# hid turned without TensorE: moved between partitions by DMA, turned in 32x32 blocks by VectorE

## The chip, the core and the metric

The kernel runs on one core of one Trainium2 chip. The metric is the device time of one execution in microseconds (us). The core has five engines that run side by side, each through its own instructions in order: TensorE (PE, with its weight loads listed apart as PEld), VectorE (DVE), ScalarE (ACT), GpSimd (POOL) and SyncE (SP). SP only issues DMAs here. All DMAs, whoever issues them, are carried by the same 16 DMA engines of the core.

## The reference

One layer of an encoder is computed for two groups of 1024 tokens of width 1024: a mixer (mLSTM heads and neighbourhood attention), and then a mixture of 16 experts in which each expert picks the 128 tokens of a group that suit it best. The change touches only the experts:

```
xe  = xf[idx]                                    # 128 tokens of each group, for each expert
hid = silu(xe @ w_gate[e]) * (xe @ w_up[e])      # (128, 1024) for each group
ye  = (hid @ w_down[e]) * gate
y   = zeros.at[idx].add(ye)
```

All three weights of an expert are 1024 x 1024 in float32. The output is x + gate2 * RMSNorm(y).

## The kernel before

The part before the experts (function `front`) takes the first 1235 us and is not touched. In it GpSimd loads the tile `fr_v` (line 906) by DMAs onto 120 or 80 partitions, whose source has as its outermost dimension 3 or 2 rows of the grid, with 40 runs of 512 B each that follow each other in HBM. The experts (function `experts`) are computed one after another. For each expert TensorE makes three products, GATE, UP and DOWN. Each has 128 tokens of two groups as rows (GROUPS = 2) and 1024 columns, so that four PSUM banks of 128 x 512 (BK = 4) hold one product; there are two such sets of banks, which alternate (j).

Every float32 operand is split into a high and a low part of the type fp32r, and each product is made of three: hi x hi, hi x lo, lo x hi. A weight comes in four pieces of 1 MB (NP = 4): a piece is 256 rows of the weight, as 128 partitions x 2 rows. A piece goes through these steps:

- SP loads it into its slot of `wf` (line 2225), once VectorE has split the piece that was in the slot before;
- ScalarE writes `w_hi` (line 2367), once the piece has landed and TensorE is done with the piece four pieces earlier;
- VectorE writes `w_lo` (line 2492);
- TensorE makes 24 matmuls from it (line 2630).

So pieces pass in a fixed order: UP of expert e, GATE of e+1, DOWN of e, UP of e+1. The order is written out by hand in `body` of each engine; nothing is scheduled by a planner. Experts 0 to 7 run in a hardware loop (`over_experts`), 8 to 15 are written out. From expert 9 on each expert also carries a "window" of up to four units of output work: POOL loads rows of y and x1 (lines 2302 and 2303), ScalarE squares, VectorE scales and adds, POOL stores.

A product needs its left operand with the contracted index on the partitions. `hid` is made with tokens on the partitions, and so it has to be turned before DOWN. Before the change `turn_h` does that on TensorE: 16 transposes of 128 x 128 into PSUM (line 2641), in the middle of GATE of e+1, whereafter ScalarE writes `h_hi` from PSUM (line 2374) and VectorE `h_lo` (line 2498). The input rows `xe` are turned in the same way by `turn_x` (same line 2641) in the middle of UP. `silu` (line 2384) and `multiply` (line 2508) make `hid`.

Of the kernel before, what the change touches and what calls it, by code (L numbers as in the profile page):

```python
# [2088 lines left out]
def experts(nc, io):  # L2089
# [25 lines left out]
    mats = [io[f"w_expert_{n}"].rearrange("e (q a p) n -> e q p a n", p=P, a=PIECE) for n in ("gate", "up", "down")]  # L2115
    with ExitStack() as ctx:
# [54 lines left out]
        hid_ready = s.sem("hid_ready")  # L2171
        h_turned = s.sem("h_turned")
# [43 lines left out]
        def is_last(e, n=1):  # L2216
            return isinstance(e, int) and e >= NE - n

        @block.sync
        def _(sp):  # L2220
            def load(e, step, first=False):
                for q in range(NP):
                    if not first:
                        sp.wait_ge(w_lo_ready, ONE + piece(e, step, q) - NP + 1)
                    sp.dma_start(wf[:, q, :, :], mats[step][e, q]).then_inc(w_loaded[q], 16)

            load(0, GATE, True)

            for g in range(GROUPS):  # L2230
                sp.wait_ge(first_x[g], 16)

            def body(e, j):
                load(e, UP)
                if isinstance(e, int) and e == FIRST:
                    for g in range(GROUPS):
                        sp.dma_start(rows[:, g, :], mod_row[g, GATE2:GATE2 + 1, :].to_broadcast([P, D])).then_inc(rows_loaded, 16)
                if not is_last(e):
                    load(e + 1, GATE)
                load(e, DOWN)  # L2240

            over_experts(sp, body)
# [117 lines left out]
        def _(act):  # L2360
# [60 lines left out]
            def body(e, j):  # L2421

                ns = window(e)
                if is_last(e):
                    split(e, DOWN, range(0, 2))
                    turned_out(e, (h_hi, j), h_turned, h_hi_ready, range(0, 2))
                    split(e, DOWN, range(2, NP))
                    for n in ns:
                        square(n)
                    turned_out(e, (h_hi, j), h_turned, h_hi_ready, range(2, BK))  # L2430
                else:
                    split(e + 1, GATE, range(0, 2))
                    turned_out(e + 1, (x_hi[:, 1 - j], 1 - j), x_turned, x_hi_ready)
                    split(e + 1, GATE, range(2, NP))

                    split(e, DOWN, range(0, 1))
                    for n in ns[0:2]:
                        square(n)
                    split(e, DOWN, range(1, 2))
                    turned_out(e, (h_hi, j), h_turned, h_hi_ready)  # L2440
                    split(e, DOWN, range(2, NP))
# [17 lines left out]
        def _(dve):  # L2459
# [39 lines left out]

            def multiply(e, j, bs=range(BK)):  # L2500
# [42 lines left out]
            def body(e, j):  # L2543
                ns = window(e)
                if is_last(e):
                    multiply(e, j, range(0, 2))
                    split(e, DOWN, range(0, 2))
                    turned_out(e, h_hi, h_lo, j, h_hi_ready, h_ready, range(0, 2))
# [4 lines left out]
                    turned_out(e, h_hi, h_lo, j, h_hi_ready, h_ready, range(2, BK))  # L2553
                    for n in ns:
                        result(n)
                else:
                    split(e + 1, GATE, range(0, 2))
                    turned_out(e + 1, x_hi[:, 1 - j], x_lo[:, 1 - j], 1 - j, x_hi_ready, x_ready)
                    split(e + 1, GATE, range(2, NP))
                    multiply(e, j)  # L2560
                    split(e, DOWN, range(0, 1))
                    for n in ns[0:2]:
                        mean(n)
                    split(e, DOWN, range(1, 2))
                    turned_out(e, h_hi, h_lo, j, h_hi_ready, h_ready)
# [40 lines left out]
        def _(pe):  # L2606
# [58 lines left out]
            def body(e, j):  # L2665
                first, second = range(0, 2), range(2, NP)
                pe.wait_ge(silu_ready, ONE + e * BK + 2)
                if is_last(e):
# [7 lines left out]
                    pe.wait_ge(h_ready, ONE + e * BK + 2)  # L2676
# [3 lines left out]
                    pe.wait_ge(h_ready, ONE + e * BK + BK)  # L2680
                    for b in bs[1]:
                        products(e, DOWN, j, h_hi, h_lo, bs=range(b, b + 1))
                else:
# [10 lines left out]
                    pe.wait_ge(h_ready, ONE + e * BK + BK)  # L2694
# [83 lines left out]
```

## Time and profile before

| | |
|---|---|
| median of 3 runs | 2404.12 us (2403.29 to 2409.57) |
| span of the profiled execution | 2402.6 us |
| its time outside the span | not listed apart; the median run is 1.5 us above the span |
| PE busy | 2296.1 us, 96% |
| DVE, ACT, POOL busy | 1208.7, 1103.8, 603.2 us |
| experts | from about 1235 us to the end |
| one expert, experts 1 to 14 | 68.85 us |
| loads of `wf` for GATE, UP, DOWN, issue to landing | 4.9, 4.9, 5.8 us |

In the page, a line of part 5 gives a group of instructions: how often, the sum of busy time, the mean of one in ns, and behind the second bar how long its engine stood idle just before, and what ended that. A matmul's own duration (389 ns) is longer than the distance from one to the next (227 ns), since they are pipelined: what a matmul costs is read from starts.

### The profile page before, as it was taken

What the parts mean: (1) busy time and instruction counts of PE and PEld (TensorE: products, weight loads), DVE (VectorE), ACT (ScalarE), POOL (GpSimd) and SP (SyncE); (2) the same over time, 40 slices, a digit from 0 to 9 for tenths busy, and PEclk for the clock granted to TensorE, in tenths of its full rate; (3) what the DMA queues carried; (4) which work ended last, traced back from release to release, by engine and by line L of the source; (5) the groups of instructions that cost most, each with busy time, mean ns of one, the idle gap of its engine ahead of it and who ended that gap; (6) DMA issues with size and microseconds to landing.
All of it is one profiled execution on the core that took longest, in us unless ns stands there. A gap on an engine that the chain in (4) does not pass through costs nothing. (4 is left out here: it accounts for less than half of the span.)

```text
span 2402.6 us, 35196 instructions
## 1 busy us (share of the span) xinstructions
PE 2296.1 (96%) x13583; PEld 1915.1 (80%) x13583; DVE 1208.7 (50%) x1881; ACT 1103.8 (46%) x1828; POOL 603.2 (25%) x676
## 2 busy tenths in 40 slices
PE   6999999999999999999947999999999999999997
PEld 4679989777899897667736888888888888888886
DVE  3222334554413346665566555544445556666655
ACT  4223444655433436665543444444444455555552
POOL 3004342443133324430021011111110122222434
PEclk9999999999999999999978999999999999999999
DMA  8835445658454459764547566666666678888785
GB/s 319 259 107 182 145 160 185 191 150 185 122 194 141 162 177 249 228 180 158 170 189 263 204 211 221 214 226 210 207 203 231 216 268 309 322 308 291 284 302 175
DMA packets 239040, 511.49 MB, mean 213 GB/s; under 512 B 36981, under 2 KB 128005, under 8 KB 235825
## 3 DMA queue, kind: packets, MB, share of 16 engines
q1 hardware_dynamic: 190960, 394.78, 49.0%
q0 software_dynamic: 47936, 114.77, 16.0%
q8 instruction: 93, 1.52, 0.3%
q14 instruction: 51, 0.41, 0.1%
HBM read 415.32 MB, written 93.69 MB: 212 GB/s over the span
## 5 line engine op out<-in xcount | busy, mean ns | idle before, releaser
L2492 DVE TENSOR_TENSOR moe_w_lo<-moe_wf,moe_w_hi 128x2048 fp32r<-128x2048 f32 x192 | 439.5, 2292 | 456.6 <-ACT moe_w_hi L2367 450.0
L2367 ACT ACTIVATE moe_w_hi<-moe_wf 128x2048 fp32r<-128x2048 f32 x192 | 367.8, 1916 | 551.4 <-PE moe_acc L2630 550.5
L2630 PE MATMUL moe_acc<-moe_w_hi,moe_x_hi 128*128 128x512 f32 x1024 | 401.7, 392 | 0.9 <-DVE moe_x_lo L2498 0.6
L2630 PE MATMUL moe_acc<-moe_w_hi,moe_x_lo 128*128 128x512 f32 x1024 | 398.9, 390 | 0.0
L2630 PE MATMUL moe_acc<-moe_w_lo,moe_x_hi 128*128 128x512 f32 x1024 | 398.4, 389 | 0.0
L2630 PEld LDWEIGHTS moe_acc<-moe_w_hi,moe_x_hi 128*128 128x128 f32 x1024 | 192.3, 188 | 40.7 <-DVE moe_x_lo L2498 0.8
L2630 PEld LDWEIGHTS moe_acc<-moe_w_hi,moe_x_lo 128*128 128x128 f32 x1024 | 192.2, 188 | 40.3
L2630 PEld LDWEIGHTS moe_acc<-moe_w_lo,moe_x_hi 128*128 128x128 f32 x1024 | 192.4, 188 | 38.9
L1793 PE MATMUL banks<-fr_w_hi,fr_h_hi 128*128 128x256 f32 x768 | 223.2, 291 | 0.0
L1793 PE MATMUL banks<-fr_w_lo,fr_h_hi 128*128 128x256 f32 x768 | 217.0, 283 | 0.0
L1793 PE MATMUL banks<-fr_w_hi,fr_h_lo 128*128 128x256 f32 x768 | 216.9, 282 | 0.0
L1784 PE MATMUL banks<-fr_h_hi,fr_w_hi 128*128 128x512 f32 x496 | 204.3, 412 | 1.9 <-DVE fr_h_lo L1381 1.1
L2630 PE MATMUL moe_acc<-moe_w_hi,moe_h_hi 128*128 128x512 f32 x512 | 199.3, 389 | 0.0
L2630 PE MATMUL moe_acc<-moe_w_hi,moe_h_lo 128*128 128x512 f32 x512 | 199.2, 389 | 0.0
L2630 PE MATMUL moe_acc<-moe_w_lo,moe_h_hi 128*128 128x512 f32 x512 | 199.2, 389 | 0.0
L1784 PE MATMUL banks<-fr_h_hi,fr_w_lo 128*128 128x512 f32 x496 | 194.2, 392 | 0.0
L1784 PE MATMUL banks<-fr_h_lo,fr_w_hi 128*128 128x512 f32 x496 | 193.7, 390 | 0.0
L1030 ACT ACTIVATE fr_stage<-banks 128x512 f32<-128x512 f32 (+1 forms) x114 | 67.3, 590 | 271.9 <-PE banks L1784 146.2
L1362 DVE TENSOR_TENSOR fr_w_lo<-fr_w_raw,fr_w_hi 128x1024 fp32r<-128x1024 f32 x56 | 73.6, 1316 | 208.3 <-ACT fr_w_hi L1018 208.3
L906 POOL DMA_DIRECT2D fr_v<-scratch_vov x224 | 156.5, 740 | 81.9 <-PE banks L1963 80.6
L1793 PEld LDWEIGHTS banks<-fr_w_hi,fr_h_hi 128*128 128x128 f32 x768 | 146.8, 191 | 4.9 <-issue 4.8
L1793 PEld LDWEIGHTS banks<-fr_w_lo,fr_h_hi 128*128 128x128 f32 x768 | 147.0, 191 | 0.1
(294 smaller groups left out, 4083.4 us busy)
## 6 DMA issues: line engine op xcount, KB each, us to landing
moe_wf<-in_w_expert_gate SPq DMA_DIRECT2D x64, 1024.0 KB, 4.9
moe_wf<-in_w_expert_up SPq DMA_DIRECT2D x64, 1024.0 KB, 4.9
moe_wf<-in_w_expert_down SPq DMA_DIRECT2D x64, 1024.0 KB, 5.8
fr_w_raw<-in_w_units SPq DMA_DIRECT2D x28, 1024.0 KB, 7.2
fr_bias<-in_na_bias SPq DMA_DIRECT2D x16, 1520.0 KB, 11.1
fr_a_w<-in_w_ada POOLq DMA_DIRECT2D x16, 1024.0 KB, 9.0
scratch_qk_t<-fr_stage SPq DMA_DIRECT2D x64, 256.0 KB, 2.5
scratch_vov<-fr_stage SPq DMA_DIRECT2D x96, 128.0 KB, 2.2
```

The costliest lines, as they stand in the source:

```text
L906: pool.dma_start(v[j][p0:CHUNK, CH_AT[rb] + n, :], v_view[2, m, r0:r0 + k, cols_, :]).then_inc(nv_loaded[j], 16)
L1030: nc.scalar.activation(out, product, ACT.Copy).then_inc(evac_done, 1)
L1362: nc.vector.tensor_tensor(w_lo[:, h % 2, k, :], w_raw[:, h % 2, k, :], w_hi[:, h % 2, k, :].bitcast(F32), ALU.subtract).then_inc(w_lo_read ...
L1784: mm = nc.tensor.matmul(ps[:, b % 2, :], w[x1][:, slot, k, a * P:(a + 1) * P], h[x2][:, k, t * HALF:(t + 1) * HALF], start=start, stop=stop)
L1793: mm = nc.tensor.matmul(ps[:, b % 2, part * QW:(part + 1) * QW], h[x1][:, k, tile:tile + P], w[x2][:, slot, k, :], start=(k == 0 and i == ...
L2367: nc.scalar.activation(w_hi[:, q, :, :], wf[:, q, :, :], ACT.Copy).then_inc(w_hi_ready, 1)
L2492: nc.vector.tensor_tensor(w_lo[:, q, :, :], wf[:, q, :, :], w_hi[:, q, :, :].bitcast(F32), ALU.subtract).then_inc(w_lo_ready, 1)
L2630: mm = nc.tensor.matmul(acc[:, j, b, :], x[:, g, k, :], w[:, q, a, h * HALF:(h + 1) * HALF], start=(k == 0 and i == 0), stop=(k == KC - 1 ...
```

## The change

`hid` is turned for experts 0 to 14 without TensorE. SP issues 32 DMAs for each expert (`move_h`, 16 for each group): each moves 32 partitions (a quarter of the tokens) x 256 columns (1 KB, a quarter of the columns) from `hid` to another quarter of the partitions of `h_quarters`. Then partition quarter u holds the columns u*256 to u*256+255 of all tokens, and one VectorE instruction for each group turns 32 x 32 blocks into `h_raw`. ScalarE and VectorE make `h_hi` and `h_lo` from that, from SBUF, in two instructions of 128 x 1024 each instead of four of 128 x 512 from PSUM. `h_quarters` and `h_raw` lie in the memory of `h_hi` and `h_lo`.

The turned `hid` then has its columns in another order over the partitions, and the rows of `w_down` are loaded in the same order: partition u*32+c of piece q holds the rows u*256 + q*64 + 2c and the one behind it, two rows of 4 KB that follow each other in HBM. The last expert keeps the old way.

```
@@ weights
-    mats = [io[f"w_expert_{n}"].rearrange("e (q a p) n -> e q p a n", p=P, a=PIECE) for n in ("gate", "up", "down")]
+    by_chunk = [w.rearrange("e (q a p) n -> e q p a n", p=P, a=PIECE) for w in weights]
+    by_quarter = [w.rearrange("e (u q c a) n -> e q u c a n", u=4, q=NP, c=QT) for w in weights]
@@ SP
+                    rows = by_quarter[step] if step == DOWN and e < NE - 1 else by_chunk[step]
+                    sp.dma_start(wf[:, q, :, :], rows[e, q]).then_inc(w_loaded[q], 16)
+            def move_h(e):
+                for g in range(GROUPS):
+                    sp.wait_ge(hid_ready, ONE + e * BK + 2 * g + 2)
+                    for t in range(4):
+                        for u in range(4):
+                            sp.dma_start(h_quarters[u * QT:(u + 1) * QT, g, t, :],
+                                         hid[t * QT:(t + 1) * QT, g, u * 2 * P:(u + 1) * 2 * P]).then_inc(h_moved[g], 16)
...
-                load(e, DOWN)
+                    load(e, DOWN, qs=range(NP - 1))
+                    move_h(e)
+                    load(e, DOWN, qs=range(NP - 1, NP))
@@ ScalarE
+            def h_out(e):
+                for g in range(GROUPS):
+                    act.wait_ge(h_turned, ONE + e * GROUPS + g + 1)
+                    nc.scalar.activation(h_hi[:, g, :, :], h_raw[:, g, :, :], ACT.Copy).then_inc(h_hi_ready, 1)
...
-                    act.wait_ge(h_turned, ONE + e * BK)
+                    for g in range(GROUPS):
+                        act.wait_ge(h_moved[g], e * 16 * 16)
@@ VectorE
+            def turn_h(e):
+                for g in range(GROUPS):
+                    dve.wait_ge(h_moved[g], (e + 1) * 16 * 16)
+                    columns = h_quarters[:, g, :, :].rearrange("p t n -> p (t n)").rearrange("p (b c a) -> p b a c", c=QT, a=PIECE)
+                    turned = h_raw[:, g, :, :].rearrange("p m (t r) -> p t m r", t=4)
+                    nc.vector.transpose(turned, columns).then_inc(h_turned, 1)
...
-                    split(e + 1, GATE, range(2, NP))
+                    split(e + 1, GATE, range(2, 3))
                     multiply(e, j)
+                    split(e + 1, GATE, range(3, NP))
+                    turn_h(e)
                     split(e, DOWN, range(0, 1))
+                    h_out(e)
@@ TensorE
-                    products(e + 1, GATE, 1 - j, x_hi[:, 1 - j], x_lo[:, 1 - j], first)
-                    turn_h(e, j)
-                    products(e + 1, GATE, 1 - j, x_hi[:, 1 - j], x_lo[:, 1 - j], second)
-                    pe.wait_ge(h_ready, ONE + e * BK + BK)
+                    products(e + 1, GATE, 1 - j, x_hi[:, 1 - j], x_lo[:, 1 - j])
+                    pe.wait_ge(h_ready, ONE + (e + 1) * GROUPS)
                     products(e, DOWN, j, h_hi, h_lo)
```

SP's order for one of the written-out experts, before (`moe_wf` is the tile of loaded weights):

```order
L2225 DMA moe_wf<-in_w_expert_up 128x2x1024 x4
L2225 DMA moe_wf<-in_w_expert_gate 128x2x1024 x4
L2225 DMA moe_wf<-in_w_expert_down 128x2x1024 x4
L2225 DMA moe_wf<-in_w_expert_up 128x2x1024 x4
```

and now:

```order
L2235 DMA moe_wf<-in_w_expert_up 128x2x1024 x4
L2235 DMA moe_wf<-in_w_expert_gate 128x2x1024 x4
L2235 DMA moe_wf<-in_w_expert_down 128x1x2048 x3
L2242 DMA moe_h_quarters<-moe_hid 32x256 x32
L2235 DMA moe_wf<-in_w_expert_down 128x1x2048
L2235 DMA moe_wf<-in_w_expert_up 128x2x1024 x4
```

The 32 small DMAs stand between the third and the fourth piece of DOWN, and a piece of DOWN has one run of 2048 values for each partition instead of two of 1024.

VectorE's order for one of the last experts, from GATE's second half to the output units, before:

```order
L2492 TENSOR_TENSOR moe_w_lo<-moe_wf,moe_w_hi 128x2048 x2
L2508 TENSOR_TENSOR moe_hid<-moe_hid,moe_acc 128x512 x4
L2492 TENSOR_TENSOR moe_w_lo<-moe_wf,moe_w_hi 128x2048
L2512 TENSOR_SCALAR moe_parts<-moe_parts 128x1 x2
L2492 TENSOR_TENSOR moe_w_lo<-moe_wf,moe_w_hi 128x2048
L2498 TENSOR_TENSOR moe_h_lo<-moe_acc,moe_h_hi 128x512 x4
```

and now:

```order
L2522 TENSOR_TENSOR moe_w_lo<-moe_wf,moe_w_hi 128x2048
L2551 TENSOR_TENSOR moe_hid<-moe_hid,moe_acc 128x512 x4
L2522 TENSOR_TENSOR moe_w_lo<-moe_wf,moe_w_hi 128x2048
L2535 STREAM_TRANSPOSE moe_h_raw<-moe_h_quarters 128x4x8x32 x2
L2522 TENSOR_TENSOR moe_w_lo<-moe_wf,moe_w_hi 128x2048
L2540 TENSOR_TENSOR moe_h_lo<-moe_h_raw,moe_h_hi 128x1024 x2
```

The product of silu and UP now stands ahead of the split of GATE's last piece, the two transposes behind that split, and `h_lo` behind the split of DOWN's first piece.

TensorE's order in the middle of GATE, before, with the 16 transposes of `hid`, which are gone now (in their place matmul follows matmul):

```order
L2630 MATMUL moe_acc<-moe_w_hi,moe_x_hi 128x512
L2630 MATMUL moe_acc<-moe_w_lo,moe_x_hi 128x512
L2630 MATMUL moe_acc<-moe_w_hi,moe_x_lo 128x512
L2641 MATMUL moe_acc<-moe_parts,moe_hid 128x128 x16
L2630 MATMUL moe_acc<-moe_w_hi,moe_x_hi 128x512
```

The 48 matmuls of GATE behind these transposes now stand directly behind the first 48.

## Rows read from the trace of the kernel before

**Rows 1.** Page, part 5: VectorE's weight split, and TensorE's first group of matmuls

```profile
L2492 DVE TENSOR_TENSOR moe_w_lo<-moe_wf,moe_w_hi 128x2048 fp32r<-128x2048 f32 x192 | 439.5, 2292 | 456.6 <-ACT moe_w_hi L2367 450.0
L2630 PE MATMUL moe_acc<-moe_w_hi,moe_x_hi 128*128 128x512 f32 x1024 | 401.7, 392 | 0.9 <-DVE moe_x_lo L2498 0.6
```

**Rows 2.** Window over expert 6: length, PE, PEld, DVE, ACT, POOL, PEclk, DMA, GB/s

```profile
1721.80:1790.60 68.80, 68.80 (x321) 57.44 (x320) 34.69 (x24) 31.15 (x28) 9.88 (x7) 1.00 0.66 213
```

**Rows 3.** Timeline of TensorE in that expert: start, us, engine, line, operation

```profile
1745.37 0.39 PE L2630 MATMUL moe_acc<-moe_w_hi,moe_x_hi 128*128 128x512 f32 x1
...
1756.26 1.91 PE L2641 MATMUL moe_acc<-moe_parts,moe_hid 128*128 128x128 f32 x16
1757.92 0.48 PE L2630 MATMUL moe_acc<-moe_w_hi,moe_x_hi 128*128 128x512 f32 x1
1758.24 0.40 PE L2630 MATMUL moe_acc<-moe_w_lo,moe_x_hi 128*128 128x512 f32 x1
```

**Rows 4.** Timeline of VectorE and SP around the end of UP

```profile
1749.73 2.48 DVE L2508 TENSOR_TENSOR moe_hid<-moe_hid,moe_acc 128x512 f32<-128x512 f32 x4
```

```profile
1731.72 0.37 SPq L2225 DMA_DIRECT2D moe_wf<-in_w_expert_down  x1
1744.46 0.37 SPq L2225 DMA_DIRECT2D moe_wf<-in_w_expert_down  x1
```

**Rows 5.** SP's DMA issues: min/median/max ns, and two in a row by the timeline

```profile
L2225 SPq DMA_DIRECT2D moe_wf<-in_w_expert_down x64: 367/370/373, 1318.6 to 2349.2; - x64
L519 SPq DMA_DIRECT2D scratch_ends<-fr_b x4: 421/426/607, 108.4 to 555.7; - x4
108.41 1.07 SPq L519 DMA_DIRECT2D scratch_ends<-fr_b  x2
899.96 4.84 SPq L549 DMA_DIRECT2D fr_mx_raw<-scratch_mix_t  x4
```

**Rows 6.** DMA issues: KB each, median us from issue to landing

```profile
scratch_vov<-fr_stage SPq DMA_DIRECT2D x96, 128.0 KB, 2.2
fr_v<-scratch_vov POOLq DMA_DIRECT2D x160, 60.0 KB, 6.9
fr_v<-scratch_vov POOLq DMA_DIRECT2D x64, 40.0 KB, 7.7
```

**Rows 7.** Groups by form: VectorE and ScalarE operations on 128 x 1024 values

```profile
L2526 DVE TENSOR_TENSOR moe_fx<-moe_fx,moe_fy 128x1024 f32<-128x1024 f32 x26 | 31.9, 1226 | 2.3 <-issue 0.5
L1373 DVE TENSOR_SCALAR fr_x<-fr_x,fr_rms 128x1024 f32<-128x1024 f32 x16 | 11.3, 768 | 3.4 <-POOL fr_rms L792 3.4
L1670 DVE TENSOR_TENSOR fr_nd<-fr_nd,fr_rr 128x1024 f32<-128x1024 f32 x8 | 18.4, 2305 | 0.2
L2407 ACT ACTIVATE moe_zero<-moe_fy 128x1024 f32<-128x1024 f32 x26 | 27.6, 1063 | 12.7 <-DMA moe_fy<-scratch_y,moe_parts 10.9
```

**Rows 8.** DMA view: 1746.9 to 1749.9, then the whole of expert 6

```profile
DMA packets 318, 1.24 MB, mean 412 GB/s; under 512 B 16, under 2 KB 16, under 8 KB 318
```

```profile
DMA packets 3840, 14.68 MB, mean 213 GB/s; under 512 B 256, under 2 KB 256, under 8 KB 3840
```

**Rows 9.** A load of `fr_v` by GpSimd; 1035.30 to 1035.62; 0.32 us of a weight piece

```profile
1033.84 1.44 POOL L906 DMA_DIRECT2D fr_v<-scratch_vov  x2
```

```profile
DMA packets 63, 0.01 MB, mean 44 GB/s; under 512 B 60, under 2 KB 60, under 8 KB 63
```

```profile
DMA packets 13, 0.05 MB, mean 166 GB/s; under 512 B 0, under 2 KB 0, under 8 KB 13
```

**Rows 10.** Windows around two changes of TensorE's clock (columns as in Rows 2)

```profile
1273.37:1276.10 2.73, 2.73 (x13) 2.73 (x14) 2.49 (x7) 0.30 (x2) 0.30 (x2) 0.50 0.02 6
2387.30:2392.30 5.00, 0.00 (x0) 0.00 (x0) 2.84 (x4) 0.72 (x2) 1.94 (x3) 1.00 0.26 107
2392.40:2402.00 9.60, 0.00 (x0) 0.00 (x0) 0.00 (x0) 0.00 (x0) 0.31 (x1) 0.50 0.14 55
```

**Rows 11.** Timeline of GpSimd in expert 12: the first of the four loads that start the window

```profile
2152.06 0.59 POOL L2302 DMA_DIRECT2D moe_fy<-scratch_y  x1 [0.93 <-DMA scratch_y<-moe_ye,moe_parts]
```

More of the change, by code:

```diff
@@ L2146, in experts @@
         hid = s.sb("hid", [P, GROUPS, D])
+        with nc.sbuf_tensor("moe_h_quarters", [P, GROUPS, 4, D // 4], F32) as h_quarters:
+            pass
         h_hi = s.sb("h_hi", [P, GROUPS, KC, P], F32R)
+        with nc.sbuf_tensor("moe_h_raw", [P, GROUPS, KC, P], F32) as h_raw:
+            pass
         h_lo = s.sb("h_lo", [P, GROUPS, KC, P], F32R)
@@ L2171, in experts @@
         hid_ready = s.sem("hid_ready")
+        h_moved = [s.soft_sem(f"h_moved{g}") for g in range(GROUPS)]
+        last_h_turned, last_h_hi_ready, last_h_ready = (s.sem(f"last_h_{n}") for n in ("turned", "hi_ready", "ready"))
         h_turned = s.sem("h_turned")
@@ L2239, in body @@
                     load(e + 1, GATE)
-                load(e, DOWN)
-            over_experts(sp, body)
+                if is_last(e):
+                    load(e, DOWN)
+                else:
+                    load(e, DOWN, qs=range(NP - 1))
+                    move_h(e)
+                    load(e, DOWN, qs=range(NP - 1, NP))
+            for e in range(NE):
+                body(e, e % 2)
         @block.gpsimd
@@ L2429, in body @@
                         square(n)
-                    turned_out(e, (h_hi, j), h_turned, h_hi_ready, range(2, BK))
+                    turned_out(0, (h_hi, j), last_h_turned, last_h_hi_ready, range(2, BK))
                 else:
@@ L2436, in body @@
                     split(e, DOWN, range(0, 1))
+                    h_out(e)
                     for n in ns[0:2]:
                         square(n)
-                    split(e, DOWN, range(1, 2))
-                    turned_out(e, (h_hi, j), h_turned, h_hi_ready)
-                    split(e, DOWN, range(2, NP))
+                    split(e, DOWN, range(1, NP))
                     silu(e + 1, 1 - j)
@@ L2498, in turned_out, with h_out @@
                     nc.vector.tensor_tensor(part(lo), acc[:, j, b, :], part(hi).bitcast(F32), ALU.subtract).then_inc(done, 1)
+            def turn_h(e):
[4 more added lines that the diff above has]
+                    nc.vector.transpose(turned, columns).then_inc(h_turned, 1)
+            def h_out(e):
+                for g in range(GROUPS):
+                    dve.wait_ge(h_hi_ready, ONE + e * GROUPS + g + 1)
+                    nc.vector.tensor_tensor(h_lo[:, g, :, :], h_raw[:, g, :, :], h_hi[:, g, :, :].bitcast(F32),
+                                            ALU.subtract).then_inc(h_ready, 1)
             def multiply(e, j, bs=range(BK)):
@@ L2547, in body @@
                     split(e, DOWN, range(0, 2))
-                    turned_out(e, h_hi, h_lo, j, h_hi_ready, h_ready, range(0, 2))
+                    turned_out(0, h_hi, h_lo, j, last_h_hi_ready, last_h_ready, range(0, 2))
                     multiply(e, j, range(2, BK))
@@ L2552, in body @@
                         mean(n)
-                    turned_out(e, h_hi, h_lo, j, h_hi_ready, h_ready, range(2, BK))
+                    turned_out(0, h_hi, h_lo, j, last_h_hi_ready, last_h_ready, range(2, BK))
                     for n in ns:
@@ L2564, in body @@
                     split(e, DOWN, range(1, 2))
-                    turned_out(e, h_hi, h_lo, j, h_hi_ready, h_ready)
                     for n in ns[0:2]:
@@ L2650, in turn_h @@
                 pe.wait_ge(hid_ready, ONE + e * BK + bs[-1] + 1)
-                turn(hid, j, h_turned, bs)
+                turn(hid, j, last_h_turned, bs)
             bs = [range(2 * g, 2 * g + 2) for g in range(GROUPS)]
```

14 lines of the change are left out of this document (8 added, 6 removed).

## The prediction

> **What bounds the kernel now.** I read the window over one expert first. In the 68.80 us of expert 6 TensorE is busy for 68.80 at the full clock, and the other engines for half of it or less [rows 2]. The groups by line agree: the first group of matmuls stood idle for 0.9 us in 1024, while VectorE and ScalarE wait for TensorE [rows 1]. So from GATE of expert 0 to the last DOWN the time is the sum of what TensorE does, at 0.2267 us from matmul to matmul, and every step of the change is asked two things: does it take starts off TensorE, and does TensorE now wait.
>
> **What goes.** The 16 transposes of `hid` start at 1756.26 and the next matmul at 1757.92, 1.66 us, and that matmul takes 0.32 us to the next start instead of 0.23 [rows 3]. One turn costs 1.75 us, and 15 of the 16 experts lose it: 26.3 us. Nothing hid it, so all of it is gain if nothing is late in its place.
>
> **What must be in time.** I count from the end of UP, at 1745.37 [rows 3], called 0. GATE of e+1 is 96 matmuls, 21.8 us. `h_ready` used to be met well before it; now DOWN starts at +21.8 only if the whole way has been gone: product in VectorE, 32 DMA issues, landing, transpose, split of DOWN's first piece, two `h_lo`.
> - Product: four operations in 2.48 us [rows 4], 0.62 each. It no longer stands behind GATE's last split, so group 0 is done at about +1.6 and group 1 at +2.8.
> - Issues: the nearest row is a DMA of 32 partitions on SP. It takes 421 ns at best, and two in a row 1.07 us with one of them at 607 [rows 5], which leaves 0.04 between them: 0.465 us each, 14.9 us for 32. From below, a load of 128 partitions issues in 0.37 [rows 5], 0.41 with the gap: 13.1. I take 0.465, same partitions. The last one is issued at +16.1 to +16.6.
> - Landing: 2.2 us from issue for 128 KB, the nearest [rows 6]; here 32 KB that stay in SBUF, so 1.5 to 2.2, I take 2.2: +18.3.
> - Transposes of 128 x 1024: not in this trace. Bounds are 0.77 us (a one-input operation) and 2.31 (one with a spread operand); I take 1.2, the plain 128 x 1024 with two inputs [rows 7], since the operand here steps over two values.
> - Behind the second transpose on VectorE stand the split of DOWN's first piece, 2.29 [rows 1], and two `h_lo` at 1.23 [rows 7]. ScalarE's `h_hi`, 1.06, lies beside the split.
>
> With loads as they are this gives 18.3 + 1.2 + 2.3 + 2.4 = +24.2: TensorE waits 2.4 us, more than the 1.75 it saves.
>
> **The loads of DOWN.** A piece has the same 1 MB, but its source is now a pattern of four blocks (u), each of 32 partitions, 256 KB in one run, where it was 128 rows. What does the trace show of a source with a small outermost dimension? `fr_v` is loaded by GpSimd with 3 or 2 outermost rows onto 120 or 80 partitions. Of the one issued at 1033.84, when nothing else moves, 3 packets of 4 KB started in 0.32 us (63 less 60 small ones), though it has 120 partitions to write; in the first 0.32 us of a weight piece 13 started [rows 9]. And 40 KB with 2 rows land in 7.7 us, 60 KB with 3 rows in 6.9 [rows 6]: time goes by what each row's share is, not by the bytes. I read it so: the outermost dimension of the source sets how many of the 16 DMA engines carry a DMA. These are GpSimd's DMAs, and none of SP's in this trace has such a pair of patterns; that SP does the same is my main assumption. Then a piece of DOWN is carried by 4 engines.
>
> The Trainium skill, DMA: Bandwidth & Descriptors, section "Why a DMA increments its semaphore by 16 and not by 1", says it outright: both kinds of DMA use the largest number up to 16 that divides the slowest dimension of source and of destination. By it the number here is 4; without it the sum would be the one that ends in +24.2. The trace of `fr_v` agrees with it.
>
> What 4 engines make of it: in the busiest stretch 16 engines move 412 GB/s [rows 8], 25.75 each. A piece has 256 KB for each of 4, 10.2 us, instead of 64 KB for each of 16, 2.5.
> - Three pieces stand ahead of the small DMAs. The first is issued at 1731.72, -13.65, and the third at 1744.46, -0.9 [rows 4]. The first packets come 1.0 us later, since one follows the other without a gap: -12.7 + 30.5 = +17.9.
> - The same engines carry their share of gather and scatter. An expert moves 14.68 MB [rows 8], of which 12 pieces are 12.58, so 2.1 MB are GpSimd's; most of it (I take 1.8 MB, an estimate from the places of these DMAs in the expert) falls into this stretch: 1.8 / 16 / 25.75 GB/s = 4.4 us. Third piece done: +22.2.
 So some of the 32 are issued only afterwards. +25.7 if none, +29 if ten; I take +27.
> - Transpose 1.2, split 2.3, two `h_lo` 2.4: +32.9. TensorE waits 32.9 - 21.8 = 11.1 us.
>
> **The clock.** After the last matmul TensorE was still granted 1.00 for the 5 us to 2392.3, then 0.50 (1.2 of 2.4 GHz), and after a long pause it worked for its first 2.73 us at 0.50 [rows 10]. A wait of 11 us is longer than the 5.3 after which the level fell, so DOWN begins at half speed for some 2.7 us: 1.4 us lost. A wait of 2.4 us costs nothing of this kind.
>
> **Experts 9 to 14.** GpSimd issues four loads of 512 KB at the start of each window, at 2152.06 in expert 12 [rows 11], 6.4 us before the end of its UP (2134.89 + 23.56). They lie ahead of or between the third piece: 2 MB / 16 / 25.75 = 5.1 us more, a wait of 16.2.
>
> **The sum.** Experts 0 to 8: 11.1 + 1.4 - 1.75 = 10.75, times 9: 97. Experts 9 to 14: 16.2 + 1.4 - 1.75 = 15.85, times 6: 95. Together +192 on the span of 2402.6: 2595, and 1.5 more for what lies between span and median run: 2596 us. The last expert is unchanged.
>
> Check of the loads as a whole: each of the four engines carries in an expert 4 MB / 4 + 8 MB / 16 + (2.1 + 1.0) / 16, 1.77 MB, 69 us, and 84 with the window. The expert would last 79.6 and 84.7. So they are nearly saturated, and in the window the time could not be shorter by another route.
>
> What costs nothing: the fourth piece of DOWN comes late (issued at about +27, landed +39), and TensorE needs it three pieces after DOWN's start, +49. ScalarE's new order and the smaller reads (SBUF for PSUM) lie beside DOWN. SP's unrolled loop takes register steps away from an engine that waits.
>
> **Range of this case.** From below: no blocked issue, half of GpSimd's share, a transpose of 0.77: wait 7.1, 12.2 in windows, sum +133, 2537. From above: in expert 6 the engines are busy 0.66 of the time [rows 2] where 14.68 MB at 25.75 each need 0.52; if the three pieces are stretched by the same 1.27, 8.2 us, and the transpose takes 2.3: waits 20.4 and 25.5, +332, 2736.
>
> **Rivals.**
> 1. SP's loads use 16 engines all the same, and the chain of 32 issues is what is late. For it: the rows on `fr_v` are of another issuer, and the destination has 128 partitions. Wait 2.4, no clock loss: 15 x (2.4 - 1.75) = +10, 2414 us; with a transpose of 2.3, 2430.
> 2. The other side: 16 engines, and the way ends in time. It decides at +21.8, that is 2.4 us less than my sum. 0.41 for an issue gives 1.8 of them, a landing in 1.5 another 0.7. Then 2404.1 - 26.3 = 2378 us. Against it: each of these values is the lower bound of its row.
> 3. Four engines, but `hid` and the pieces do not queue behind each other as I have it, and only saturation counts: 9 experts at their wait of rival 1, +0.65 each, and 6 at 84 instead of 68.85, +15: 2502 us.
>
> **Chances.** Four engines as summed 0.67, rival 3 0.08, rival 1 0.15 (of which 0.03 within 0.3%), rival 2 0.10 (0.01 of it within). 0.3%, 7 us, is about what a measurement of this kernel tells from no change. So slower 0.87, same 0.04, faster 0.09. The predicted time is that of the likeliest, 2596 us; its own range 2537 to 2736. The range of 8 in 10 takes in rivals 3 and 1: 2405 to 2710.
>
> **What would show it.** In the profile after: `moe_wf<-in_w_expert_down` lands in some 12 us or more, while the other two stay near the 4.9 of the table; TensorE waits for `h_lo` at its first matmul of DOWN, 15 times, over 10 us each; the clock's row falls to 0.50 there; VectorE's largest idle time is ahead of the transposes, ended by the DMA of `h_quarters`. If DOWN's pieces land in 5 us, the step on four engines is wrong and rival 1 or 2 holds, told apart by whether that wait is there at all. If they land late and TensorE waits under 5 us, it is the queueing that I have wrong. The transposes' mean tells whether 1.2 us stood.

## The result, and the profile after

The changed kernel takes 2881.01 us (2866.86 to 2885.66, 4 runs), the kernel before 2403.82 us beside it: a ratio of 1.1972, interval 1.1941 to 1.2002. The prediction was 2596 us with a range to 2710. The sign was right; the loss is 477 us, not 192.

The page of the kernel after, parts 1 to 5: clock and DMA shares, packets, chain, and the groups that answer to [rows 1].

```profile
PEclk9999999999999999979888898889887977967968
...
DMA packets 253682, 527.26 MB, mean 183 GB/s; under 512 B 43940, under 2 KB 150324, under 8 KB 242784
...
SPq L2242 20%; PE moe_acc L2675 16%; DMA moe_h_quarters<-moe_hid 2%; DMA moe_wf<-in_w_expert_down 2%; DMA moe_fy<-scratch_y 1%; DMA out<-moe_fx 1%; PE moe_acc L2686 1%; DVE moe_w_lo L2522 1%; DVE moe_hid L2551 1%; ACT moe_w_hi L2391 1%; DMA
...
L2675 PE MATMUL moe_acc<-moe_w_hi,moe_h_hi 128*128 128x512 f32 x512 | 215.2, 420 | 450.1 <-DVE moe_h_lo L2540 449.8
L2391 ACT ACTIVATE moe_w_hi<-moe_wf 128x2048 fp32r<-128x2048 f32 x192 | 362.8, 1915 | 558.7 <-DMA moe_wf<-in_w_expert_down 349.1
...
L2675 PE MATMUL moe_acc<-moe_w_hi,moe_x_hi 128*128 128x512 f32 x1024 | 401.4, 392 | 9.8 <-DVE moe_w_lo L2522 9.5
...
L2535 DVE STREAM_TRANSPOSE moe_h_raw<-moe_h_quarters 128x1024 f32<-128x1024 f32 x30 | 37.4, 1245 | 588.0 <-DMA moe_h_quarters<-moe_hid 588.0
```

The groups of GATE and UP are as before except for one wait near the end. What is new is 450 us in which TensorE waits for `h_lo` at the first matmul of DOWN. `h_lo` waits for the transposes, and these for the moves of `hid`. The chain goes back through SP's issues (L2242, a fifth of the span).

One expert, number 5, by window: the columns are those of [rows 2]. The second row holds the last of GATE and the start of the wait, the third lies inside the wait, the fourth is the start of DOWN.

```profile
1770.61:1862.60 91.99, 65.08 (x287) 53.34 (x286) 32.30 (x23) 27.14 (x25) 7.75 (x7) 0.85 0.60 159
...
1815.00:1820.00 5.00, 1.06 (x5) 0.56 (x3) 0.00 (x0) 0.00 (x0) 0.00 (x0) 0.91 0.33 110
1820.00:1825.00 5.00, 0.00 (x0) 0.00 (x0) 0.00 (x0) 0.00 (x0) 0.00 (x0) 0.50 0.35 124
1842.87:1848.00 5.13, 5.13 (x15) 4.12 (x16) 4.27 (x2) 0.11 (x1) 0.00 (x0) 0.66 1.04 184
```

The expert lasts 92 us instead of 68.8 [rows 2]. In the empty stretch from 1820 to 1825 the DMA share is 0.35 at 124 GB/s, where 16 engines moved 412 GB/s [rows 8].

The timelines of SP, VectorE and TensorE over the same expert, against [rows 3, 4]. UP ends, and GATE of expert 6 begins, at 1794.14; this is 0 in what follows.

```profile
1780.52 13.23 SPq L2235 DMA_DIRECT2D moe_wf<-in_w_expert_down  x3
1795.65 37.45 SPq L2242 DMA_DIRECT2D moe_h_quarters<-moe_hid  x32
1833.14 0.60 SPq L2235 DMA_DIRECT2D moe_wf<-in_w_expert_down  x1
```

```profile
1794.34 2.48 DVE L2551 TENSOR_TENSOR moe_hid<-moe_hid,moe_acc 128x512 f32<-128x512 f32 x4 [1.14 <-PE moe_acc L2675]
...
1834.09 1.25 DVE L2535 STREAM_TRANSPOSE moe_h_raw<-moe_h_quarters 128x1024 f32<-128x1024 f32 x1 [35.07 <-DMA moe_h_quarters<-moe_hid]
1837.04 1.25 DVE L2535 STREAM_TRANSPOSE moe_h_raw<-moe_h_quarters 128x1024 f32<-128x1024 f32 x1 [1.71 <-DMA moe_h_quarters<-moe_hid]
1838.21 2.25 DVE L2522 TENSOR_TENSOR moe_w_lo<-moe_wf,moe_w_hi 128x2048 fp32r<-128x2048 f32 x1
1840.38 2.35 DVE L2540 TENSOR_TENSOR moe_h_lo<-moe_h_raw,moe_h_hi 128x1024 fp32r<-128x1024 f32 x2
```

```profile
1842.87 0.79 PE L2675 MATMUL moe_acc<-moe_w_hi,moe_h_hi 128*128 128x512 f32 x1 [26.81 <-DVE moe_h_lo L2540]
```

SP needs 37.45 us for 32 issues; the second half of `hid` lands at +42.9, DOWN starts at +48.7 and TensorE has waited 26.8. From the transposes on everything takes what was forecast.

The DMA view of DOWN's pieces: 0.32 us inside the first piece, then three stretches, one for each of the first three pieces. A stretch goes from a piece's first 8-KB packet to the next piece's first, the last one to the end of the third piece. A piece is 128 packets of 8 KB, and their number in a stretch is the total less those "under 8 KB". Behind the totals stands what each queue did in a stretch (q0 is GpSimd's, q1 SP's): packets, MB, and their time as a share of 16 engines.

```profile
DMA packets 4, 0.03 MB, mean 102 GB/s; under 512 B 0, under 2 KB 0, under 8 KB 0
```

```profile
DMA packets 589, 2.46 MB, mean 132 GB/s; under 512 B 78, under 2 KB 126, under 8 KB 463
q0 software_dynamic: 389, 1.38, 40.3%
...
DMA packets 587, 1.53 MB, mean 100 GB/s; under 512 B 144, under 2 KB 408, under 8 KB 459
q0 software_dynamic: 59, 0.21, 4.0%
...
DMA packets 786, 1.50 MB, mean 121 GB/s; under 512 B 222, under 2 KB 658, under 8 KB 658
q1 hardware_dynamic: 786, 1.50, 35.8%
```

Four packets start in 0.32 us, where 13 of 4 KB did before [rows 9]. The three stretches (1784.20, 1802.85, 1818.15 to 1830.55) are 18.6, 15.3 and 12.4 us long. In all of expert 5, GpSimd's queue was busy for 11.6% of 92 us, 10.7 us on each of 16 engines (first line). In the kernel before, the same 576 packets took 12.5% of the 68.8 us of expert 6, 8.6 us on each (second line):

```profile
q0 software_dynamic: 576, 2.10, 11.6%
...
q0 software_dynamic: 576, 2.10, 12.5%
```

The packets of four bytes count the engines too: each engine that carries a DMA leaves one. Before there were 36,981 under 512 B; 480 moves on 16 engines add 7,680; the sum is 44,661, and 43,940 is 721 less: 12 for each of the 60 changed pieces, and one that I can't place. Four engines, each time.

### The profile page after: what moved, and what is told of

The parts are those of the page before. It is cut to its first block, busy times and chain, and to the rows that moved or that the text cites. A ratio compares the mean times of both kernels' runs of the same rounds, so it can differ in the third digit from the quotient of the medians.

```text
span 2879.3 us, 34966 instructions
## 1 busy us (share of the span) xinstructions
PE 2309.1 (80%) x13343; PEld 1913.3 (66%) x13343; DVE 1234.6 (43%) x1881; ACT 1097.3 (38%) x1798; POOL 600.2 (21%) x676
## 2 busy tenths in 40 slices
DMA packets 253682, 527.26 MB, mean 183 GB/s; under 512 B 43940, under 2 KB 150324, under 8 KB 242784
## 4 chain that ended last, share of the span: by engine, by line
SPq 20%; PE 17%; DMA 9%; DVE 5%; issue 3%; ACT 2%; POOL 1%; DVEq 1%; ACTq 0%; POOLq 0%
SPq L2242 20%; PE moe_acc L2675 16%; DMA moe_h_quarters<-moe_hid 2%; DMA moe_wf<-in_w_expert_down 2%; DMA moe_fy<-scratch_y 1%; DMA out<-moe_fx 1%; PE moe_acc L2686 1%; DVE moe_w_lo L2522 1%; DVE moe_hid L2551 1%; ACT moe_w_hi L2391 1%; DMA moe_fy<-scratch_y,moe_parts 1%; DMA out<-moe_fx,moe_parts 1%; DVE moe_h_lo L2540 1%; DVEq L2564 0%; DVE moe_fx L2569 0%
## 5 line engine op out<-in xcount | busy, mean ns | idle before, releaser
L2675 PE MATMUL moe_acc<-moe_w_hi,moe_h_hi 128*128 128x512 f32 x512 | 215.2, 420 | 450.1 <-DVE moe_h_lo L2540 449.8
L2675 PEld LDWEIGHTS moe_acc<-moe_w_hi,moe_h_hi 128*128 128x128 f32 x512 | 103.9, 203 | 479.4 <-DVE moe_h_lo L2540 266.1
L2535 DVE STREAM_TRANSPOSE moe_h_raw<-moe_h_quarters 128x1024 f32<-128x1024 f32 x30 | 37.4, 1245 | 588.0 <-DMA moe_h_quarters<-moe_hid 588.0
L2675 PE MATMUL moe_acc<-moe_w_lo,moe_h_hi 128*128 128x512 f32 x512 | 211.2, 413 | 0.0
L2675 PE MATMUL moe_acc<-moe_w_hi,moe_h_lo 128*128 128x512 f32 x512 | 209.7, 410 | 0.0
L2404 ACT ACTIVATE moe_h_hi<-moe_h_raw 128x1024 fp32r<-128x1024 f32 x30 | 31.7, 1056 | 447.5 <-DVE moe_h_raw L2535 447.5
## 6 DMA issues: line engine op xcount, KB each, us to landing
fr_bias<-in_na_bias SPq DMA_DIRECT2D x16, 1520.0 KB, 10.7
```

The lines of the kernel that those rows point to most:

```text
L2404: nc.scalar.activation(h_hi[:, g, :, :], h_raw[:, g, :, :], ACT.Copy).then_inc(h_hi_ready, 1)
L2535: nc.vector.transpose(turned, columns).then_inc(h_turned, 1)
L2675: mm = nc.tensor.matmul(acc[:, j, b, :], x[:, g, k, :], w[:, q, a, h * HALF:(h + 1) * HALF], start=(k == 0 and i == 0), stop=(k == KC - 1 ...
```

## The experiments

Each kernel is the one named, with the edit shown. Times are medians; the kernel before took 2402.9 to 2403.2 us beside them.

**1. The change with 16 engines per piece.** The source has 128 rows outermost; `hid`'s columns are turned to fit.

```
- by_quarter: "e (u q c a) n -> e q u c a n"      (4 blocks outermost)
+ by_quarter: "e (p q a) n -> e q p a n"          (128 rows outermost)
- columns:    "p (b c a) -> p b a c"              (a step of 8 bytes)
+ columns:    "p (t c m) -> p t m c"              (a step of 32 bytes)
```

> The change with one thing undone: a piece of DOWN is read with 128 rows outermost in its source instead of 4 blocks, so 16 engines can carry it; the 32 moves, the VectorE transposes and all orders stay. Output is the reference's. Theory A (four engines per DOWN piece are the cause): the 8-KB packets of DOWN start 13 or more in 0.32 us, the completion packets of 4 bytes rise by 12 more per DOWN piece, the pieces are done when the moves are issued, and only the chain of issues is late. In the unblocked tail of the changed kernel's chain a move took 0.633 us from issue to issue, so 32 are 20.3 us: +1.6 + 20.3 + 2.2 + 1.2 + 2.3 + 2.4 = +30.0 after UP's end, a wait of 8.2 us, with 1.4 of clock less 1.75: 15 x 7.9 = +118, about 2520 us (2414 if an issue were 0.465). Theory B (the 32 small moves themselves hold SP and the queue, whoever carries the pieces): SP stays blocked in its issues for over 35 us, the wait stays above 20 us, the time 2800 or more.

2540.27 us, ratio 1.0568 (1.0550 to 1.0585). Its page, and 0.32 us of a piece of DOWN:

```profile
DMA packets 254402, 527.26 MB, mean 208 GB/s; under 512 B 44660, under 2 KB 151044, under 8 KB 243504
...
L2675 PE MATMUL moe_acc<-moe_w_hi,moe_h_hi 128*128 128x512 f32 x512 | 215.5, 421 | 118.3 <-DVE moe_h_lo L2540 118.3
...
L2535 DVE STREAM_TRANSPOSE moe_h_raw<-moe_h_quarters 128x1024 f32<-128x1024 f32 x30 | 62.2, 2073 | 242.9 <-DMA moe_h_quarters<-moe_hid 242.9
...
moe_h_quarters<-moe_hid SPq DMA_DIRECT2D x480, 32.0 KB, 1.9
```

```profile
DMA packets 13, 0.11 MB, mean 333 GB/s; under 512 B 0, under 2 KB 0, under 8 KB 0
```

```profile
1721.37 20.17 SPq L2242 DMA_DIRECT2D moe_h_quarters<-moe_hid  x32
```

The 720 small packets are back, 13 packets start in 0.32 us, SP is no longer blocked, and 341 of the 477 us are gone. Theory A holds, 20 us above its number. What stays is rival 1 of the prediction, with a larger price: 32 issues take 20.2 us, not 14.9, and a transpose 2.07.

**2. The loads alone.** The kernel before, with the changed source of DOWN's pieces and TensorE's turn of `hid`.

```
+ by_quarter = io["w_expert_down"].rearrange("e (u q c a) n -> e q u c a n", u=4, q=NP, c=P // 4)
- sp.dma_start(wf[:, q], mats[step][e, q])
+ rows = by_quarter if step == DOWN and not is_last(e) else mats[step]
+ sp.dma_start(wf[:, q], rows[e, q])
```

> The kernel before with one part of the change alone: pieces of DOWN for experts 0 to 14 are read with 4 blocks outermost in their source (SP's loop unrolled for it). TensorE turns hid as before, there are no moves. The rows of w_down then stand in another order than those of hid, so the product is not the reference's; nothing else is left out. Theory A (the pieces are carried by 4 engines, 12 to 21 us each): the third and fourth pieces of DOWN come after TensorE wants them. Piece 1 starts near -12.7 after UP's end and with no moves between, four pieces at 14 us end near +43; DOWN starts at +23.5 and wants piece q at +23.5 + 5.4 q, that is piece 3 at +39.8 less the split of 2.3: a wait of some 6 us per expert, 15 x 6 = +90, about 2490 us; experts 9 to 14 wait longer than 0 to 8. Theory B (the loads are harmless by themselves and only the moves behind them hurt): within 1% of the kernel before, 2404 us. Theory C (the loads account for nearly all): above 2750 us.

2739.25 us, ratio 1.1385 (1.1360 to 1.1409). Its groups and waits:

```profile
L2633 PE MATMUL moe_acc<-moe_w_hi,moe_h_hi 128*128 128x512 f32 x512 | 229.2, 448 | 266.2 <-DVE moe_h_lo L2501 185.9
```

```profile
ACT moe_w_hi L2370 <- DMA moe_wf<-in_w_expert_down: 650.6, 60, 20.2
```

The kind of Theory A was right and its size was not: +336, where I had +90; Theory B is out, and Theory C's 2750 us is nearly reached. The loads alone cost 336 us, and the change with its loads put right (experiment 1, with slower transposes and without TensorE's turns) 137; together 473, and the whole change costs 477. Waits overlap and needn't add up, so I draw nothing from that sum. The largest part is not the moves but the pattern of the loads. All 60 splits wait for DOWN's DMAs.

**3. Fewer, larger moves.** Experiment 1, with both groups in one DMA, and DOWN's first split ahead of the transposes.

```
+ sp.wait_ge(hid_ready, ONE + e * BK + 4)
- sp.dma_start(h_quarters[u*QT:(u+1)*QT, g, t, :], hid[t*QT:(t+1)*QT, g, u*2*P:(u+1)*2*P])   (32 of them)
+ sp.dma_start(h_quarters[u*QT:(u+1)*QT, :, t, :], hid[t*QT:(t+1)*QT, :, u*2*P:(u+1)*2*P])   (16 of them)
- turn_h(e); split(e, DOWN, range(0, 1)); h_out(e)
+ split(e, DOWN, range(0, 1)); turn_h(e); h_out(e)
```

> As the run with 128 rows outermost, and further: both groups of hid go in one DMA (16 moves of 32 partitions x 2 KB in two runs of 1 KB, instead of 32), and DOWN's first piece is split by VectorE ahead of the transposes instead of behind them. Output is the reference's. Theory A (number of issues on SP sets the landing): 16 x 0.633 = 10.1 us from group 1's product at +2.8, landing 2.2: +15.1, transposes 2.4, two h_lo 2.4: +19.9, ahead of GATE's end at +21.8; no wait for h_lo, TensorE saves 1.75 us 15 times: 2404 - 26 = 2378 us. Theory B (an issue's cost goes with its rows, so a DMA of 64 rows costs twice): the chain is as long as with 32, +25 to +26 at the last h_lo: wait about 4 us, 2440 us. Theory C (the moves wait in the queue behind UP's or DOWN's pieces): above 2450 us.

2426.84 us, ratio 1.0104 (1.0087 to 1.0122).

```profile
1669.64 10.20 SPq L2241 DMA_DIRECT2D moe_h_quarters<-moe_hid  x16
```

```profile
PE moe_acc L2673 <- DVE moe_h_lo L2538: 25.9, 6, 7.3
```

An issue of 64 rows costs 0.64 us like one of 32, so the number of issues counts: the moves take 10.2 us instead of 20.2. The split's new place hides up to 2.3 us more; the two edits were not run apart. Experts 0 to 8 show no wait and last 67.1 us, 1.75 less than before: there Theory A holds. From expert 9 on, where GpSimd loads and stores rows for the output, `h_lo` is late six times, and the splits of weights (`w_lo`) three times, 11.4 us; that wasn't forecast, and with it the run stays 49 us above Theory A.

**4. The moves ahead of pieces 2 to 4**, in the change as it is.

```
- load(e, DOWN, qs=range(NP - 1)); move_h(e); load(e, DOWN, qs=range(NP - 1, NP))
+ load(e, DOWN, qs=range(1));      move_h(e); load(e, DOWN, qs=range(1, NP))
```

> The change with one order altered: only DOWN's first piece is issued ahead of the 32 moves, and pieces 2 to 4 behind them (before: three ahead, one behind). Output is the reference's. Theory A (the moves are late because SP's issues block behind three pieces of DOWN on four engines): SP's issues are blocked only for what is left of the first piece, moves land by about +25, but the pieces behind them, some 12 to 15 us each on four engines, start at about +22 and end near +35, +47, +60; DOWN starts near +32 and then waits inside itself for its pieces, 10 to 20 us in all; the wait for h_lo falls below 12 us, and the wait moves to the splits of DOWN; time 2800 to 2950 us, near the changed kernel's 2881, because the four engines stay the bound. Theory B (saturation of the four engines plays no part, only the queueing of the moves does): waits for h_lo fall to about 10 us and nothing comes in their place: 2560 to 2620 us.

2946.76 us, ratio 1.2271 (1.2251 to 1.2292). TensorE's waits:

```profile
PE moe_acc L2675 <- DVE moe_w_lo L2522: 268.1, 46, 11.9
PE moe_acc L2675 <- DVE moe_h_lo L2540: 155.1, 15, 16.8
```

The waits for `h_lo` fall from 450 to 155, and 268 us of waits for DOWN's later pieces take their place. Moving the queue about helps nothing while a piece takes 12 us or more. Theory B is out.

**5. The scatter without addition**, in the change.

```
- pool.indirect_dma_start(io["y"], ..., ye[:, g, :], None, compute_op=ALU.add)
+ pool.indirect_dma_start(io["y"], ..., ye[:, g, :], None)
```

> The change with one thing altered: GpSimd's scatter of an expert's result writes its rows instead of adding to them, so what several experts give to one row isn't summed (that part of the computation is changed). An adding packet of 4 KB takes 327 ns on its DMA engine, a plain one about 160; there are 256 of them per expert, 16 on each engine. Theory A (the four engines that carry DOWN are never idle while its pieces are under way, so every us of GpSimd's share on them lengthens the way): 16 x 0.167 = 2.7 us less per expert, 15 x 2.7 = 40, about 2840 us, and DOWN's first two pieces shorter together by about that. Theory B (the scatter is no part of what makes DOWN's pieces last 15 to 18 us): 2881 us within 0.3%. Theory C (adding packets hold up the engine by far more than they are busy): below 2780 us.

2847.78 us, ratio 1.1861 (1.1843 to 1.1880): 33 us less than the change, of 40 expected. In expert 5 GpSimd's queue took 8.0% of 92.6 us, 7.4 us on each engine instead of 10.7:

```profile
q0 software_dynamic: 576, 2.10, 8.0%
```

So part of the time of DOWN's pieces is GpSimd's share on the same engines. Theories B and C are out.

**6. Experiment 3 with the moves behind DOWN's first piece** (the edit of 4).

> The run with both groups in one DMA (16 engines per DOWN piece, 16 moves), with one order altered: the 16 moves are issued behind DOWN's first piece, and pieces 2 to 4 behind them. Output is the reference's. Theory A (in experts 9 to 14 the moves queue behind DOWN's pieces 2 and 3, which share the engines with GpSimd's four window loads: they land 4.5 to 5 us later there, and that is the whole loss): the waits of 3.7 to 5.4 us for h_lo there go or fall under 1 us, with their clock loss of 1.8; all 15 experts at 67.1 us instead of 68.85: 2403 - 26 = 2377 us, at most 2390. Theory B (the window loads hold up the moves wherever they stand in SP's order, or the pieces that now come later are late): 2410 to 2430 us.

2402.20 us, ratio 0.9994 (0.9984 to 1.0003). Neither theory's number. The waits for `h_lo` fall from 25.9 to 5.9 us, those for `w_lo` stay (11.4 in experiment 3, 12.9 now):

```profile
PE moe_acc L2673 <- DVE moe_w_lo L2520: 12.9, 6, 7.5
PE moe_acc L2673 <- DVE moe_h_lo L2538: 5.9, 3, 3.7
```

**7. Four DMAs per piece**, in the change: same rows, same places, only cut.

```
+ for u in range(4):
+     sp.dma_start(wf[u * QT:(u + 1) * QT, q], rows[e, q, u]).then_inc(w_loaded[q], 16)
```

> The change with one thing altered: each piece of DOWN is loaded by four DMAs of 32 partitions (256 KB), one for each block of rows, instead of one DMA with the four blocks outermost. Layout, transposes, moves and orders stay. Output is the reference's. Theory A (the one DMA's outermost dimension of 4 is what confines it to four engines): the 8-KB packets start 13 or more in 0.32 us again and pieces take 3 to 5 us; the transposes stay at 1.25 us (8-byte steps), where the kernel with 128 rows outermost had 2.07 (32-byte steps), so the way to h_lo is 0.8 to 1.6 us shorter than there: wait 6.5, period 75.2, about 2520 us against 2540. Theory B (the layout of the rows, four runs of 256 KB at 1 MB from each other, is what is slow, however it is cut into DMAs): 2800 us or more.

2554.24 us, ratio 1.0635 (1.0619 to 1.0651).

```profile
DMA packets 257283, 527.28 MB, mean 207 GB/s; under 512 B 47540, under 2 KB 153924, under 8 KB 246384
...
L2541 DVE STREAM_TRANSPOSE moe_h_raw<-moe_h_quarters 128x1024 f32<-128x1024 f32 x30 | 37.4, 1245 | 282.3 <-DMA moe_h_quarters<-moe_hid 282.3
```

The layout of the rows in memory is not to blame, Theory B is out: cut into four DMAs, each of 32 outermost rows, the same bytes no longer cost 327 us. The small packets say 16 engines for each (36,981 + 7,680 + 180 x 16 = 47,541, one more than the page has). The transposes are short again, but the kernel isn't faster than experiment 1: experts 0 to 8 wait 6.8 to 8.0 us, but four of the last six 12.5 to 14.4. Why the four DMAs do worse there stays open.

**8 and 9. Orders in the late experts.** Experiment 9 is 6 with one more piece of DOWN and of UP split ahead of the work on GpSimd's rows in experts 10 to 14; experiment 8 has the four DMAs of 7 besides.

```
  h_out(e)
+ split(e, DOWN, range(1, 2))
  for n in ns[0:2]: mean(n)                (ScalarE alike, with square)
- split(e, DOWN, range(1, 2))
+ split(e, DOWN, range(2, 3))
  for n in ns[0:2]: result(n)
- split(e, DOWN, range(2, NP)); split(e + 1, UP, range(0, 2))
+ split(e, DOWN, range(3, NP)); split(e + 1, UP, range(0, 3))
```

> The run with 16 moves behind DOWN's first piece, with two things more. (1) A piece of DOWN as four DMAs of 32 partitions, so the transposes step over 8 bytes and not 32 (1.25 us each instead of 2.07). (2) In experts 10 to 14 ScalarE and VectorE split one more piece of DOWN and of UP before the work on rows that GpSimd loaded. Output is the reference's. Theory A (the 9 experts without window work save 1.75 us each, and what is lost in experts 9 to 15 are the h_lo waits of 0.9 to 3.9 us, the w_lo waits of 0.8 to 1.5 us inside DOWN, their clock loss of 1 to 2, and one wait of 7.5 us in UP of expert 15, all from the order on VectorE and the 1.65 us of the two slower transposes): the waits go, all 15 experts at 67.1 us, 2403 - 26 = 2377 us, at most 2385. Theory B (GpSimd's own chain in a window, scatter, loads, stores, takes about 68 us and sets the period there, whatever the order on VectorE): experts 10 to 14 stay at 68 to 70 us and the tail keeps a wait of 5 us or more: 2395 to 2405 us.

> As the run before it, but with the layout of the run with 16 moves behind DOWN's first piece (one DMA per piece with 128 rows outermost, transposes of 2.07 us): only the order of the splits on ScalarE and VectorE in experts 10 to 14 differs from that run. Output is the reference's. Theory A (the order is what costs the waits for w_lo, the transposes those for h_lo): the 7.5 us in expert 15 and the waits inside DOWN go, the waits for h_lo of 0.9 to 3.9 us stay: 2402 less 7 to 15, 2387 to 2395 us. Theory B (GpSimd's chain sets the period): 2398 to 2405 us.

8: 2427.73 us, 1.0099 (1.0084 to 1.0115). 9: 2398.22 us, 0.9981 (0.9972 to 0.9990). 8 lies above both of its theories, 9 at the lower edge of its Theory B. TensorE's waits in 9:

```profile
PE moe_acc L2675 <- DVE moe_h_lo L2539: 8.0, 4, 4.1
PE moe_acc L2675 <- DVE moe_w_lo L2521: 5.4, 1, 5.4
```

The waits inside DOWN are gone, those at its start remain. In 8 the gather of the next expert's rows comes late (3.3 to 7.7 us between two starts on TensorE, in five experts). I read it so that the late experts have little slack on GpSimd's side, which the kernel before just covered; no run shows that by itself.

**10. Each kind of expert its own way.** Experiment 6 for experts 0 to 8, the kernel before for 9 to 14.

```
+ def moved(e): return not isinstance(e, int) or e < FIRST + 1
+ if not moved(e): turn_h(e, j)              (TensorE; orders of the kernel before on all engines)
```

> The run with 16 moves behind DOWN's first piece, for experts 0 to 8 alone; experts 9 to 14 are as in the kernel before (TensorE turns hid, rows in chunks, all pieces of DOWN in one go, its orders on ScalarE and VectorE). Output is the reference's. Theory A (what 16 moves and 16 engines per piece save is 1.75 us in each expert without window work, and all that was lost was in experts 9 to 15): 9 x 1.75 = 15.8 us under the kernel before, 2403 - 16 = 2387 us. Theory B (an expert of the one kind behind one of the other loses it again, or the tail's wait of 7.5 us comes from time saved earlier and not from the orders in the windows): 2394 to 2403 us.

2385.83 us, ratio 0.9930 (0.9916 to 0.9943): 17 us less than the kernel before. One expert of the first kind, and a line of its page:

```profile
1656.65:1723.70 67.05, 67.05 (x306) 55.73 (x305) 38.62 (x24) 31.08 (x27) 9.12 (x7) 1.00 0.72 235
```

```profile
L2689 PE MATMUL moe_acc<-moe_w_hi,moe_h_hi 128*128 128x512 f32 x512 | 199.3, 389 | 0.0
```

TensorE never waits in DOWN, the clock is full, and 9 x 1.75 = 15.8 us are the gain. Theory A holds.

## Why the prediction was right in its sign and wrong in its size

- **1.75 us saved per expert: right.** Experiments 3 and 10 show it alone, 68.8 to 67.05.
- **Four engines per piece: right**, and SP's DMAs follow it as GpSimd's did. Experiments 1 and 7 undo it in two ways; the trace agrees with the rule on the slowest dimension (the largest number up to 16 that divides it on both sides) in the Trainium skill, DMA: Bandwidth & Descriptors, section "Why a DMA increments its semaphore by 16 and not by 1", also at 32 and 128 outermost rows, both of which went to 16.
- **"Third piece done: +22.2": the step that failed.** Its last packet started at +36.1 (1830.2), 13.9 later. The first packet came at -9.9 and not -12.7: 2.8. The pieces took 46.0 us and not 30.5 + 4.4: 11.1 more.
  - GpSimd's share. I priced 1.8 MB of it at the full rate, 4.4 us. In the first two stretches its queue took 40.3% and 4.0%, 8.1 us on each engine: 3.7 more. Another 2.5 us lie ahead of the first packet: from SP's issue at 1780.52 to 1784.17 the engines were full, 69.3% with GpSimd's scatter and the rest with pieces of GATE. The price stood in the trace of the kernel before, 8.6 us for all 2.1 MB (the line above), and I did not read it. Experiment 5 shows part of why it is dear: a packet that adds takes longer.
  - The moves are not in it. Of their 1024 packets of 1 KB, 748 start within the three stretches and 276 behind them. A move goes over 16 engines, so a quarter of its packets, 256 in all, falls to the four. I read it so that these wait behind the third piece, as forecast, while the twelve other engines run ahead.
  - The other 7.4 us stay open. In the third stretch nothing of GpSimd's is under way, and the piece still takes 12.4 us and not 10.2: 128 packets at 0.32 us are 41 us of the four engines' 49.6, so they weren't busy all the time. And in the first piece the packets themselves took longer at times, with nothing else under way: from 1792 to 1795 only 24 of them start, 0.51 us each (last line below). No run tells why.

  That GpSimd and SP share the four engines is shown by the DMA view from 1787.5 to 1791.7 (first three lines):

```profile
DMA packets 56, 0.34 MB, mean 82 GB/s; under 512 B 4, under 2 KB 4, under 8 KB 24
q1 hardware_dynamic: 32, 0.26, 15.4%
q0 software_dynamic: 24, 0.08, 9.8%
...
q1 hardware_dynamic: 24, 0.20, 25.6%
```

  32 packets of 8 KB and 20 of GpSimd's 4 KB start. Together they take 25.2% of 16 engines, the whole time of four, and nothing is left for the twelve others. The Trainium skill, DMA: Bandwidth & Descriptors, section "Queues, rings and completion order", says that an engine with work from several queues takes a packet of each in turn. The trace agrees in that both queues advance on engines that are never idle; it doesn't name the engine of a packet, so the turns themselves are not shown.
- **Moves landed, +27: +42.9.** Of the 15.9 us, 13.9 come from the piece, and 2.0 from the landing behind it (6.8 instead of 4.8). I had spread that over 16 engines; by the counts above what was left was the four engines' quarter, 64 packets on each. Transposes at 1.25 (I had 1.2), split and `h_lo` stood: 5.8 us from landing to DOWN, where I had 5.9. The wait was 26.8 here and 16.3 to 26.8 over experts 0 to 8, instead of 11.1: 203 in all less 9 x 11.1 is 103 us of the miss.
- **The issue at 0.465: wrong for these DMAs, masked here.** It is 0.465 for 32 partitions out of HBM (experiment 7) but 0.63 out of SBUF, which no row of before showed. In the change it is hidden by the blocked queue; in experiment 1 it is 5.3 of the 7.9 us of mean wait.
- **The windows, +5.1: the largest miss.** The waits are 34 to 44 us in experts 9 to 14. In experiment 2, without any moves, TensorE's first wait in DOWN is 16 to 24 us there too, against 3 to 9 in experts 0 to 8. I had added the four loads to the 4.4 us of gather and scatter and moved nothing else. In expert 11 scatter, gather and four loads stood close together (below, the first and the last that GpSimd issues). SP itself issued DOWN's first piece only at -6.9 instead of -13.65, its first packet came at +1.7 instead of -12.7, and the three pieces took 50.3 us instead of 40.0. That is 24.7 of the 26.5 us by which this wait was missed; why SP is late I read from GATE's pieces, which it issues late as well (19 us for the four). The six experts wait 247 us where I had 97: 150 us of the miss.

```profile
2366.62 2.57 POOL L2314 DMA_INDIRECT scratch_y<-moe_ye,moe_parts  x1 [0.31 <-issue]
...
2382.52 0.58 POOL L2327 DMA_DIRECT2D moe_fx<-scratch_x  x1
```

- **The clock: right in kind.** It fell to 0.50 in expert 5's wait, and DOWN took 23.3 to 24.7 us in all 15 experts instead of 21.76: 33.6 in all, where I had 21: 13 us.
- **"The last expert is unchanged": wrong.** TensorE waits 9.5 us for `w_lo` in its UP, where VectorE's work on GpSimd's rows stands ahead of two splits; with that order changed (experiment 9) 5.4 us of it stay, with the late experts as before (experiment 10) it is gone: 10 us.
- 103 + 150 + 13 + 10 = 276 of the 285 missed.
- **The check of the loads as a whole** gave 69 us for the four engines, and rival 3 had 84 in the windows. An expert lasted 92 and 112 us; the loads alone (experiment 2) made it 82. I put this down to the same low price of packets, and to the four slots of `wf`, which let only four pieces be under way at a time, so that the engines can't be loaded evenly; no run tests the second.

So rival 1 is what was left with 16 engines, and rival 2, in nine of the 15 experts, what was left with fewer issues too. Rival 3 did not occur. The forecast had the path right (four engines, queue, moves, `h_lo`); its terms for that path were too small, and in the windows it started later than I had it.

## What to carry to other kernels

Read every DMA's source for its outermost dimension before counting its bytes: the same 1 MB took 12 to 19 us in expert 5 when it is 4, where it landed in 5 to 6 otherwise, and a cut into several DMAs or a reshaped source gives it back. A resource that is near its limit needs every user's price by kind of packet, read from the trace before, and not by bytes; a sum at the best rate is a lower bound there. A forecast for a loop should be made for each kind of iteration: here the same edit (experiment 3) gains 1.75 us in nine experts and loses time in the others, and the best kernel keeps both ways.

## What the runs showed of the hardware that was not expected

- SP's issue of a DMA: 0.63 us from one to the next for 32 rows of 1 KB out of SBUF, 0.64 for 64 rows, but 0.465 for 32 partitions of 8 KB out of HBM. More rows cost nothing. Source and length of row differ at once between the first and the last, so which of them costs is not shown.
- A VectorE transpose of 128 x 1024 takes 1.25 us with an operand stepping over 8 bytes, and 2.07 over 32 bytes.
- A scatter that adds is dearer for its DMA engines than one that writes: 7.4 us on each engine against 10.7 in expert 5, and 33 us over 15 experts.
